# A two-layer hybrid encoder on Trainium2: the 64 rotary dimensions of a head side by side, one product for them in a score

## The chip, the core and the metric

The kernel runs on one core of one Trainium2 chip. The metric is the device time of one execution in microseconds (us). Engines: PE multiplies matrices (PEld is its weight load), DVE and ACT work on vectors, POOL and SP here only start transfers. Each engine works through its own queue in order and waits on semaphores.

## The reference, cut to what matters

Two layers of an encoder for 256 tokens of 2048 channels. Each layer has three branches (a state-space scan with a gated linear unit, a long convolution, and attention with latent queries and keys) that are gated, lifted, merged and normalised. The change touches only the attention:

```python
def apply_rope(x, pos):
    half = x.shape[-1] // 2                      # 32 of 64
    inv = ROPE_BASE ** (-jnp.arange(half, dtype=jnp.float32) / half)
    ang = pos.astype(jnp.float32)[:, :, None, None] * inv
    cos, sin = jnp.cos(ang), jnp.sin(ang)
    x1, x2 = xf[..., :half], xf[..., half:]
    return jnp.concatenate([x1 * cos - x2 * sin, x1 * sin + x2 * cos], axis=-1)

def mla_mixer(c_q, c_kv, k_r, pos, q_norm_g, w_uq, kv_norm_g, w_ukv):   # 8 heads
    q = (rms_norm(c_q, q_norm_g) @ w_uq).reshape(bsz, L, MLA_HEADS, 128 + 64)
    q = jnp.concatenate([q[..., :128], apply_rope(q[..., 128:], pos)], axis=-1)
    kv = (rms_norm(c_kv, kv_norm_g) @ w_ukv).reshape(bsz, L, MLA_HEADS, 128 + 128)
    k = jnp.concatenate([kv[..., :128], one apply_rope(k_r) for all heads], axis=-1)
    s = jnp.einsum('bqhd,bkhd->bhqk', q, k) * scale
    return jnp.einsum('bhqk,bkhd->bqhd', jax.nn.softmax(s, axis=-1), v)
```

## The kernel before

**Weights.** All large weights pass through SBUF in blocks of 1 MB: SP loads half blocks into a ring of four slots, ACT rounds a quarter of a block to WH, DVE subtracts to get the rest, WL, and PE multiplies with both. WH and WL hold one block: each quarter can be remade only when PE has used it (`parts_used`), and PE waits for the count that DVE adds for a finished WL quarter (`w_used`). ACT's splits are L398 and L404, DVE's are L417 (one quarter) and L426 (a whole block).

**The attention stage of a layer**, in PE's order: sums of squares for the two norms (L1912); the product of the gated linear unit (L1924); twelve query tiles, then eight key tiles (`three`, L1940), one quarter of a weight block for each, 12 products of 256 columns, evicted by ACT (L1463, L1469); the first product of the convolution's filter network (L1959); two blocks of V (L1969, 24 products of 512 columns each); the second product of the filter network (L1982); then eight heads. In a head PE makes two scores, one for each half of the queries (L1995 to L1997), one gated block of the next stage (`attention`, L1723), the transposes of the probabilities (L2005), a second gated block, the product with V (L2019), and a third gated block. The softmax runs meanwhile: DVE takes the maximum (L985), ACT the exponential (L1488), DVE the division (L993).

**The rotation.** Channels lie in rows (partitions), tokens in columns. The first 32 rotary dimensions of four heads fill one tile of 128 rows, the second 32 of the same heads another: `QR` has four tiles (two halves of eight heads), `PROJ` tiles 32 and 33 hold the key's two halves, each repeated four times. `rotate` (L919) makes the two rotated halves with six DVE instructions, four products, a difference and a sum, with `cosr` and `sinr` from `ROPE`. It is called once for the key, one tile wide, after the gating of the scan's output (L915), and once for the queries, two tiles wide, between the WL quarters of the second key block and those of the first V block. A score then adds three products: 128 rows without rotation, and 32 rows for each half:

```python
r = slice(32 * (h % 4), 32 * (h % 4) + 32)
release(mm(s, qn[:, h, tok], kn[:, h, :], start=True, stop=False))               # L1995
release(mm(s, qt[r, h // 4, tok], kt[r, 0, :], start=False, stop=False))         # L1996
done(mm(s, qt[r, 2 + h // 4, tok], kt[r, 1, :], start=False, stop=True), 4 + i)  # L1997
```

PE waits for both rotations (`qk_ready`) ahead of the first head.

**DVE's order there:** the gating (L909, L915), the key's rotation, eight WL quarters (the last four of Q, the first four of K), the low part of the scan's output (`YAL`, L940), four WL quarters, the queries' rotation, four WL quarters, a wait for `qk_ready`, then for each half of V a whole block of WL (L426) and the argument of a sine of the filter network (L958 and L543 to L548), then the heads.

**POOL** starts the transfers of the scan, and in this stage three small loads (W1, W2, the features; L510 to L512) once `YAL` is made, then the filter's biases and decays.

Of the kernel before, what the change touches and what calls it, by code (L numbers as in the profile page):

```python
# [34 lines left out]
P = 128  # L35
# [79 lines left out]
LAGS = 2 * STEP - 1  # L115
DVE_STEPS, DVE_S5_STEPS = 431, 21
SETUP_STEPS = 31
# [61 lines left out]
def trunk(nc, x, blocks, lp, ln, bc, w1, w2, b3, decay, feats, pT, pos, angles, consts, out):  # L179
    with ExitStack() as ctx:  # L180
        def sb(name, cols, parts=P, dt=F32):
            return ctx.enter_context(nc.sbuf_tensor(name, [parts, cols], dt))

        def sem(name):
            return ctx.enter_context(nc.semaphore(name))
# [8 lines left out]
        LNP = sb("LNP", 2 * DT)  # L194
        ANG = sb("ANG", 2)
        ROPE = sb("ROPE", 2 * T)
# [9 lines left out]
        def area(at, n):  # L206
            return ARENA[:, at * T:(at + n) * T]
# [58 lines left out]
        PR = area(71, 2)  # L266
        ROT = area(65, 4)
        ROOTS = [area(117 + i, 1) for i in range(4)]
        PT = area(89, 4)
        KT, VV = area(93, 4), area(97, 8)  # L270
# [33 lines left out]
        def tiles(buf, at, n, w=T):  # L304
            return buf[:, at:at + n * w].rearrange("p (n w) -> p n w", w=w)
# [31 lines left out]
        sq_ready, latent_ready, qk_ready = sem("sq_ready"), sem("latent_ready"), sem("qk_ready")  # L337
        max_ready, prob_ready = sem("max_ready"), sem("prob_ready")
        arg_ready, hid_ready = sem("arg_ready"), sem("hid_ready")
        taps_ready, abs_ready, ed_ready = sem("taps_ready"), sem("abs_ready"), sem("ed_ready")  # L340
# [112 lines left out]
        def _(pool):  # L453
# [6 lines left out]
            pool.sem_inc(y4_free, 1)  # L460
            with pool.Fori(0, DEPTH) as layer:
                pool.wait_ge(xh_ready, layer * GROUPS + GROUPS)
# [44 lines left out]


                pool.wait_ge(yl_ready, layer * 4 + 1)
                pool.dma_start(W1[0:33, :], w1[layer]).then_inc(late_loaded, 16)  # L510
# [45 lines left out]
        def _(dve):  # L556
# [61 lines left out]
            for layer in range(DEPTH):  # L618
# [299 lines left out]

                def rotate(x1, x2, n, o1, o2, t1, t2):  # L919
                    cb, sb_ = (c.unsqueeze(1).to_broadcast([P, n, T]) for c in (cosr, sinr))  # L920
                    st.did(v.tensor_tensor(t1, x1, cb, ALU.mult))
                    st.did(v.tensor_tensor(t2, x2, sb_, ALU.mult)); st.wait()
                    st.did(v.tensor_tensor(o1, t1, t2, ALU.subtract)); st.wait()
                    st.did(v.tensor_tensor(t1, x1, sb_, ALU.mult))
                    st.did(v.tensor_tensor(t2, x2, cb, ALU.mult)); st.wait()
                    v.tensor_tensor(o2, t1, t2, ALU.add).then_inc(qk_ready, 1)

                kt = tiles(KT, 0, 4)
                dve.wait_ge(rope_ready, 1)

                dve.wait_ge(glu_done, layer * 8 + 8)
                rotate(PROJt[:, 32:33, :], PROJt[:, 33:34, :], 1, kt[:, 0:1, :], kt[:, 1:2, :], kt[:, 2:3, :], kt[:, 3:4, :])
                qr, qt = tiles(QR, 0, 4), tiles(QT, 0, 4)

# [7 lines left out]
                dve.wait_ge(yl_ready, layer * 4 + 1)  # L942
                tq = tiles(ROT, 0, 4)
                for q in range(4):
                    make_wl_quarter(q, layer, after_k(q))
                rotate(qr[:, 0:2, :], qr[:, 2:4, :], 2, qt[:, 0:2, :], qt[:, 2:4, :], tq[:, 0:2, :], tq[:, 2:4, :])
                for q in range(4):
                    make_wl_quarter(q, layer, after_k(4 + q))


# [371 lines left out]
        def _(act):  # L1322
# [5 lines left out]
            act.wait_ge(pos_loaded, 32)  # L1328
            a.activation(ROPE[:, T:2 * T], U[:, 4 * T:5 * T], ACT.Sin)
            a.activation(ROPE[:, 0:T], U[:, 5 * T:6 * T], ACT.Sin, bias=half_pi, scale=-1.0).then_inc(rope_ready, 1)  # L1330
# [308 lines left out]
        def _(pe):  # L1639
# [5 lines left out]
            for layer in range(DEPTH):  # L1645
# [343 lines left out]
                for h in range(HEADS):  # L1989
                    r = slice(32 * (h % 4), 32 * (h % 4) + 32)  # L1990
                    for i in range(2):
                        s = bank[4 + i][:, 0:T]
                        tok = slice(i * P, (i + 1) * P)
                        take_bank(4 + i, "mla", 1 + h)
                        release(mm(s, qn[:, h, tok], kn[:, h, :], start=True, stop=False))  # L1995
                        release(mm(s, qt[r, h // 4, tok], kt[r, 0, :], start=False, stop=False))  # L1996
                        done(mm(s, qt[r, 2 + h // 4, tok], kt[r, 1, :], start=False, stop=True), 4 + i)  # L1997

                    attention = lambda k: gated_block("lifta", k // 6, k % 6, (xh, xl), (split(YAH, WT), split(YAL, WT)), lift_a(k))
                    attention(3 * h)  # L2000
                    take_bank(6, "mla", 1 + h)
                    for i in range(2):
                        pe.wait_ge(prob_ready, layer * 16 + (h * 2 + i + 1))
                        for kt_ in range(2):
                            ins = nc.tensor.transpose(bank[6][:, kt_ * T + i * P:kt_ * T + (i + 1) * P],  # L2005
                                                      PR[:, i * T + kt_ * P:i * T + (kt_ + 1) * P], ident)
                    done(ins, 6)
                    if h == 1:

                        pe.wait_ge(yl_ready, layer * 4 + 1)  # L2010
                    attention(3 * h + 1)

                    if h == 0:
                        for b in (2, 3, 7):
                            out_of(b, "mla", 0)
                    out_of(6, "mla", 1 + h)
                    take_bank(7, "mla", 1 + h)
                    for k in range(2):
                        ins = mm(bank[7][:, 0:T], VV[:, k * W + h * P:k * W + (h + 1) * P],  # L2019
                                 PT[:, (h % 2) * 2 * T + k * T:(h % 2) * 2 * T + (k + 1) * T], start=(k == 0), stop=(k == 1))  # L2020
                    done(ins, 7)
                    attention(3 * h + 2)
# [197 lines left out]
def weight_blocks(w_in, w_glu, w_uq, w_ukv, w3, w_lift, w_ple, w_out):  # L2220
# [8 lines left out]
    out += [block_of(column_tiles(w_in, seg(c_kv, m))) for m in range(4)]  # L2229
    out += [block_of(column_tiles(w_in, np.tile(np.arange(32), 4) + c_kr + 32 * i)) for i in range(2)]  # L2230
    out += [block_of(column_tiles(w_in, seg(z, m))) for z in (a_z, b_z, c_z) for m in range(WT)]
# [3 lines left out]
    q_cols = [192 * h + np.arange(P) for h in range(HEADS)]  # L2235
    for half in range(2):
        for g in range(2):
            q_cols.append((192 * heads[4 * g:4 * g + 4] + 128 + 32 * half + np.arange(32)).reshape(-1))
    out += [block_of(sum((column_tiles(w_uq, q_cols[m + i]) for i in range(4)), [])) for m in range(0, 12, 4)]
# [28 lines left out]
def shape_constants():  # L2268
# [19 lines left out]
    inv = np.float32(10000.0) ** (-np.arange(half, dtype=np.float32) / np.float32(half))  # L2288
    angles = np.stack([np.tile(inv, 4), np.full(P, HALF_PI, np.float32)], axis=1).astype(np.float32)

# [68 lines left out]
```

## Time and profile before

| | |
|---|---|
| runs | 2487.06 us, median of 3 (2485.95 to 2489.69) |
| the profiled execution | 2488.99 us, its span 2487.4 us |
| PE | busy 2423.8 us (97%), 15208 matrix instructions |
| DVE | busy 1832.8 us (74%) |
| ACT | busy 1227.9 us (49%) |
| POOL | busy 248.8 us (10%) |
| bytes moved | 413.73 MB, 166 GB/s over the span |
| PE's mean granted clock | 0.993 of full |

The span runs from the first to the last instruction of the profiled execution; a busy share is an average over stages that differ. One fp32 product appears as two matrix instructions. Times of instructions below are counted from the span's start; the first layer's attention stage lies at about 475 to 724 us, the second's at about 1708 to 1957 us.

### The profile page before, as it was taken

To read this page: it belongs to the slowest core of one execution; us is meant where nothing else is said; L and a number is where in the kernel's file an instruction comes from. 1 tells how busy PE (TensorE), PEld (TensorE's weight loads), DVE (VectorE), ACT (ScalarE), POOL (GpSimd) and SP (SyncE) were. 2 spreads that over 40 slices of the span, in tenths; PEclk is the share of its full clock that TensorE was granted. 3 is DMA by queue.
4 is the path that set the end of the run, shared out by engine and by line. 5 is a ranking of instruction groups with operands and counts; after the bars stand their busy time and mean duration, and the time that the engine had idled before them with its cause. 6 is when DMAs were issued, how large, how long until landed. Compare 5 with 4: busy or idle time off the path is not lost.

```text
span 2487.4 us, 43446 instructions
## 1 busy us (share of the span) xinstructions
PE 2423.8 (97%) x15208; PEld 2006.4 (81%) x15208; DVE 1832.8 (74%) x3207; ACT 1227.9 (49%) x2206; POOL 248.8 (10%) x478
## 2 busy tenths in 40 slices
PE   7999999999999999999999999999999999999998
PEld 6888888887776777898778888888877777778987
DVE  7888888677787876566678888886777777755665
ACT  5455555564443434453455555555644444344534
POOL 3421212100000000000043121111000000000000
PEclk9999999999999999999999999999999999999999
DMA  7555555444453435555565555554444534355553
GB/s 257 182 179 168 177 171 178 152 162 153 148 173 119 144 111 190 188 172 175 169 209 173 174 174 173 178 178 138 164 150 150 179 110 153 114 193 190 170 178 136
DMA packets 124317, 413.73 MB, mean 166 GB/s; under 512 B 19780, under 2 KB 25978, under 8 KB 123952
## 3 DMA queue, kind: packets, MB, share of 16 engines
q1 hardware_dynamic: 107136, 390.12, 47.5%
q0 software_dynamic: 17072, 22.18, 3.1%
q8 instruction: 66, 1.08, 0.2%
q14 instruction: 43, 0.35, 0.0%
HBM read 405.01 MB, written 7.21 MB: 166 GB/s over the span
## 4 chain that ended last, share of the span: by engine, by line
PE 94%; DVE 4%; issue 1%; ACT 1%; PEldq 0%; DMA 0%; PEld 0%; DVEq 0%; POOL 0%; ACTq 0%; POOLq 0%
PE bank L1723 31%; PE bank L1765 21%; PE bank L1767 10%; PE bank L2157 7%; PE bank L1698 5%; PE bank L2077 2%; PE bank L1924 2%; PE bank L1940 2%; PE bank L2091 1%; PE bank L2057 1%; PE bank L1680 1%; PE bank L1969 1%; PE bank L1996 1%; PE bank L1827 1%; PE bank L1995 1%
## 5 line engine op out<-in xcount | busy, mean ns | idle before, releaser
L398 ACT ACTIVATE WH<-ring 128x512 fp32r<-128x512 f32 x1376 | 862.4, 632 | 1118.7 <-PE bank L1723 472.1
L426 DVE TENSOR_TENSOR WL<-ring,WH 128x512 fp32r<-128x512 f32 x860 | 579.4, 689 | 419.3 <-ACT WH L398 416.5
L1765 PE MATMUL bank<-XX,WH 128*128 128x512 f32 x2304 | 833.8, 405 | 31.2 <-DVE XX L611 15.0
L1767 PE MATMUL bank<-XX,WL 128*128 128x256 f32 x2304 | 650.5, 282 | 0.0
L1765 PEld LDWEIGHTS bank<-XX,WH 128*128 128x128 f32 x2304 | 437.0, 190 | 143.9 <-issue 33.5
L1723 PE MATMUL bank<-WH,XX 128*128 128x512 f32 x1536 | 485.2, 397 | 4.4 <-issue 2.9
L417 DVE TENSOR_TENSOR WL<-ring,WH 128x512 fp32r<-128x512 f32 x556 | 379.1, 687 | 145.4 <-ACT WH L398 130.0
L1767 PEld LDWEIGHTS bank<-XX,WL 128*128 128x128 f32 x2304 | 439.5, 191 | 0.0
L1723 PEld LDWEIGHTS bank<-WH,XX 128*128 128x128 f32 x1536 | 285.0, 188 | 80.5 <-issue 21.6
L1723 PE MATMUL bank<-WL,XX 128*128 128x512 f32 x768 | 299.7, 390 | 0.0
L1723 PEld LDWEIGHTS bank<-WL,XX 128*128 128x128 f32 x768 | 144.1, 188 | 31.2
L1698 PE MATMUL bank<-XX,WH 128*128 128x256 f32 x640 | 115.9, 284 | 1.0 <-issue 1.0
L1698 PEld LDWEIGHTS bank<-XX,WH 128*128 128x128 f32 x640 | 99.7, 192 | 1.8 <-issue 1.8
L2157 PE MATMUL bank<-WH,MIXH 128*128 128x512 f32 x256 | 100.4, 392 | 0.0
L2157 PE MATMUL bank<-WL,MIXH 128*128 128x512 f32 x256 | 99.7, 389 | 0.0
L2157 PE MATMUL bank<-WH,MIXL 128*128 128x512 f32 x256 | 99.6, 389 | 0.0
L1698 PE MATMUL bank<-XX,WL 128*128 128x256 f32 x320 | 90.5, 283 | 0.0
L506 POOL DMA_DIRECT2D ARENA<-y_scratch x128 | 66.3, 518 | 82.1 <-DMA y_scratch<-ARENA 63.7
L494 POOL DMA_DIRECT2D ARENA<-lag_scratch x128 | 65.7, 513 | 76.8 <-DMA lag_scratch<-ARENA 55.9
L476 POOL DMA_DIRECT2D ARENA<-u_scratch x128 | 67.5, 528 | 15.1 <-issue 3.3
L1698 PEld LDWEIGHTS bank<-XX,WL 128*128 128x128 f32 x320 | 61.4, 192 | 0.0
L2077 PE MATMUL bank<-ARENA,CON 128*128 128x512 f32 x128 | 57.5, 597 | 0.7 <-issue 0.6
(333 smaller groups left out, 3270.9 us busy)
## 6 DMA issues: line engine op xcount, KB each, us to landing
ring<-in_blocks SPq DMA_DIRECT2D x736, 512.0 KB, 3.3
ARENA<-in_bc POOLq DMA_DIRECT2D x2, 2048.0 KB, 9.5
ARENA<-in_decay POOLq DMA_DIRECT2D x8, 512.0 KB, 4.1
ARENA<-in_x SPq DMA_DIRECT2D x4, 512.0 KB, 8.2
u_scratch<-ARENA POOLq DMA_DIRECT2D x16, 128.0 KB, 3.2
ARENA<-u_scratch POOLq DMA_DIRECT2D x128, 16.0 KB, 2.9
ARENA<-lag_scratch POOLq DMA_DIRECT2D x128, 16.0 KB, 2.6
y_scratch<-ARENA POOLq DMA_DIRECT2D x16, 128.0 KB, 3.4
```

The lines of the kernel that those rows point to most:

```text
L398: nc.scalar.activation(wh[q], raw(which[0], q), ACT.Copy).then_inc(wh_ready[q], 1)
L417: nc.vector.tensor_tensor(wl[q], raw(which[0], q), wh[q].bitcast(F32), ALU.subtract).then_inc(w_used[slot(which[0], q // 2)], 1)
L426: vec.tensor_tensor(wl[q], raw(which[0], q), wh[q].bitcast(F32), ALU.subtract).then_inc(w_used[slot(which[0], half)], 1)
L476: pool.dma_start(split(U4[rows, m * T:(m + 1) * T], 4), by_step[s_, t]).then_inc(u4_loaded, 16)
L494: pool.dma_start(split(M[rows, :], 4), by_half[s_][:, :, (STEP - 1 - t) * 16:(2 * STEP - 1 - t) * 16]).then_inc(m_ready, 16)
L506: pool.dma_start(split(U4[rows, bass.ds(ct * T, T)], STEP), by_group[q // 2, q % 2, g_]).then_inc(y_loaded, 16)
L1698: ins = mm(o, w_, x_, start=start and i == 0 and n == 0, stop=stop and i == 7 and n == 2)
L1723: ins = mm(bank[b][:, :], x_, w_[q], start=first and n == 0, stop=last and n == 2)
L1765: ins = mm(bank[b][:, :], h, xx[:, :, k, :], start=(k == 0), stop=(k == DT - 1), skip_group_check=True)
L1767: ins = mm(bank[b][:, 0:T], l, xh[:, k, :], start=False, stop=(k == DT - 1), skip_group_check=True)
L2077: ins = mm(bank[b][:, :], tab[:, t, m * P:(m + 1) * P], ZT[:, t * W + half * CW:t * W + (half + 1) * CW], start=(t == 0), stop=(t == 1))
L2157: ins = mm(bank[b][:, :], x_[:, k, token[t]], w_[q], start=False, stop=(k == 15 and n == 2), skip_group_check=True)
```

## The change

The 64 rotary dimensions of a head now lie in 64 neighbouring rows: a query tile holds two heads, and the key's tile holds the 64 dimensions twice. A second tile holds the same with the two halves of 32 swapped. Then the rotation is x * cos + swapped * (sin with a sign by row): three DVE instructions. For the key the swapped tile comes from the projection, with its weight columns in another order. For the queries POOL copies the four blocks of 32 rows of `QR` crosswise to `QS` by four transfers from SBUF to SBUF, 128 KB each, when all query tiles are out of PSUM and the memory of `QS` is free; DVE waits for them (`qs_loaded`) ahead of the queries' rotation, which now stands behind all eight WL quarters. A score has one product of 64 rows in place of two of 32. POOL's loop over the layers is written out.

```diff
-        ANG = sb("ANG", 2)
+        ANG = sb("ANG", 3)
...
-        ROT = area(65, 4)
...
-        PT = area(89, 4)
+        PT, QS = area(89, 4), area(89, 4)
...
-            with pool.Fori(0, DEPTH) as layer:
+            for layer in range(DEPTH):
...
+                for b in (0, 1):
+                    pool.wait_ge(psum_free[b], read_out(layer, "mla", b, 5))
+                pool.wait_ge(glu_done, layer * 8 + 8)
+                for r in range(4):
+                    into, of = 32 * r, 32 * (r ^ 1)
+                    pool.dma_start(QS[into:into + 32, :], QR[of:of + 32, :]).then_inc(qs_loaded, 16)
                 pool.wait_ge(yl_ready, layer * 4 + 1)
                 pool.dma_start(W1[0:33, :], w1[layer]).then_inc(late_loaded, 16)
...
-                def rotate(x1, x2, n, o1, o2, t1, t2):
+                def rotate(x, swapped, n, o):
                     cb, sb_ = (c.unsqueeze(1).to_broadcast([P, n, T]) for c in (cosr, sinr))
-                    st.did(v.tensor_tensor(t1, x1, cb, ALU.mult))
-                    st.did(v.tensor_tensor(t2, x2, sb_, ALU.mult)); st.wait()
-                    st.did(v.tensor_tensor(o1, t1, t2, ALU.subtract)); st.wait()
-                    st.did(v.tensor_tensor(t1, x1, sb_, ALU.mult))
-                    st.did(v.tensor_tensor(t2, x2, cb, ALU.mult)); st.wait()
-                    v.tensor_tensor(o2, t1, t2, ALU.add).then_inc(qk_ready, 1)
+                    st.did(v.tensor_tensor(o, x, cb, ALU.mult))
+                    st.did(v.tensor_tensor(swapped, swapped, sb_, ALU.mult)); st.wait()
+                    v.tensor_tensor(o, o, swapped, ALU.add).then_inc(qk_ready, 1)
...
-                rotate(PROJt[:, 32:33, :], PROJt[:, 33:34, :], 1, kt[:, 0:1, :], kt[:, 1:2, :], kt[:, 2:3, :], kt[:, 3:4, :])
+                rotate(PROJt[:, 32:33, :], PROJt[:, 33:34, :], 1, kt[:, 0:1, :])
...
                 for q in range(4):
                     make_wl_quarter(q, layer, after_k(q))
-                rotate(qr[:, 0:2, :], qr[:, 2:4, :], 2, qt[:, 0:2, :], qt[:, 2:4, :], tq[:, 0:2, :], tq[:, 2:4, :])
                 for q in range(4):
                     make_wl_quarter(q, layer, after_k(4 + q))
+                dve.wait_ge(qs_loaded, layer * 64 + 64)
+                rotate(qr, qs, 4, qt)
...
-            a.activation(ROPE[:, T:2 * T], U[:, 4 * T:5 * T], ACT.Sin)
+            a.activation(ROPE[:, T:2 * T], U[:, 4 * T:5 * T], ACT.Sin, scale=ANG[:, 2:3])
...
-                    r = slice(32 * (h % 4), 32 * (h % 4) + 32)
+                    r = slice(64 * (h % 2), 64 * (h % 2) + 64)
...
-                        release(mm(s, qt[r, h // 4, tok], kt[r, 0, :], start=False, stop=False))
-                        done(mm(s, qt[r, 2 + h // 4, tok], kt[r, 1, :], start=False, stop=True), 4 + i)
+                        done(mm(s, qt[r, h // 2, tok], kt[r, 0, :], start=False, stop=True), 4 + i)
...
-    out += [block_of(column_tiles(w_in, np.tile(np.arange(32), 4) + c_kr + 32 * i)) for i in range(2)]
+    out += [block_of(column_tiles(w_in, np.tile(np.roll(np.arange(64), 32 * i), 2) + c_kr)) for i in range(2)]
...
-    for half in range(2):
-        for g in range(2):
-            q_cols.append((192 * heads[4 * g:4 * g + 4] + 128 + 32 * half + np.arange(32)).reshape(-1))
+    for h in range(0, HEADS, 2):
+        q_cols.append((192 * heads[h:h + 2] + 128 + np.arange(64)).reshape(-1))
...
+    sign = np.tile(np.repeat([-1.0, 1.0], half), 2)
```

## Rows read from the trace of the kernel before

**Rows 1.** The page's part 1: PE's busy us, share of the span, instructions.

```profile
PE 2423.8 (97%) x15208; PEld 2006.4 (81%) x15208; DVE 1832.8 (74%) x3207; ACT 1227.9 (49%) x2206; POOL 248.8 (10%) x478
```

**Rows 2.** Windows, V, then heads, first layer: us; busy by engine; clock; DMA share.

```profile
544.00:556.00 12.00, 12.00 (x52) 9.47 (x52) 7.95 (x16) 7.00 (x12) 0.00 (x0) 1.00 0.54 176
...
562.00:724.00 162.00, 162.00 (x710) 127.69 (x709) 120.77 (x253) 79.71 (x142) 1.58 (x3) 1.00 0.46 153
```

**Rows 3.** Timeline of PE, fourth head, first layer: start, us, line, operands, count.

```profile
620.36 0.69 PE L1996 MATMUL bank<-ARENA 32*128 32x256 f32 x2
620.90 0.59 PE L1997 MATMUL bank<-ARENA 32*128 32x256 f32 x2
621.42 0.70 PE L1995 MATMUL bank<-ARENA 128*128 128x256 f32 x2
622.05 0.69 PE L1996 MATMUL bank<-ARENA 32*128 32x256 f32 x2
```

**Rows 4.** Timeline of PE, both layers, gated unit to first head; [idle before].

```profile
504.70 6.42 PE L1924 MATMUL bank<-ARENA,ring 128*128 128x256 f32 x29
...
524.54 0.35 PE L1940 MATMUL bank<-CH,WH 128*128 128x256 f32 x1 [1.91 <-DVE WL L417]
...
1783.24 0.39 PE L1969 MATMUL bank<-WH,CH 128*128 128x512 f32 x1
...
1788.77 0.70 PE L1982 MATMUL bank<-ARENA 64*128 64x256 f32 x2
1789.40 0.70 PE L1995 MATMUL bank<-ARENA 128*128 128x256 f32 x2
...
1798.35 0.60 PE L2005 MATMUL bank<-CON,ARENA 128*128 128x128 f32 x4
1798.71 0.71 PE L1723 MATMUL bank<-WH,XX 128*128 128x512 f32 x2
```

**Rows 5.** Timelines of DVE and PE, seventh head, first layer: probabilities done, transposes.

```profile
690.38 0.36 DVE L993 TENSOR_SCALAR ARENA<-ARENA,SM 128x256 f32<-128x256 f32 x1
...
692.10 0.60 PE L2005 MATMUL bank<-CON,ARENA 128*128 128x128 f32 x4
```

**Rows 6.** Timeline of DVE, both layers: rotations, splits, first head's softmax.

```profile
505.19 1.23 DVE L903 TENSOR_TENSOR CL<-ARENA,CH 128x1024 fp32r<-128x1024 f32 x1
...
522.57 0.42 DVE L924 TENSOR_TENSOR ARENA<-ARENA,ROPE 128x256 f32<-128x256 f32 x1
...
523.71 2.64 DVE L417 TENSOR_TENSOR WL<-ring,WH 128x512 fp32r<-128x512 f32 x4
...
1772.89 0.69 DVE L921 TENSOR_TENSOR ARENA<-ARENA,ROPE 128x512 f32<-128x512 f32 x1
...
1778.95 0.69 DVE L417 TENSOR_TENSOR WL<-ring,WH 128x512 fp32r<-128x512 f32 x1 [0.18 <-ACT WH L404]
...
1797.32 0.35 DVE L993 TENSOR_SCALAR ARENA<-ARENA,SM 128x256 f32<-128x256 f32 x1
1797.64 2.50 DVE L426 TENSOR_TENSOR WL<-ring,WH 128x512 fp32r<-128x512 f32 x4
```

**Rows 7.** Windows behind PE's stall in either layer; columns as in rows 2.

```profile
525.90:529.30 3.40, 3.40 (x19) 3.40 (x18) 1.14 (x2) 1.35 (x4) 0.00 (x0) 0.52 0.83 265
...
1757.00:1762.00 5.00, 3.09 (x26) 2.91 (x26) 4.04 (x9) 1.92 (x4) 0.00 (x0) 1.00 0.25 85
```

**Rows 8.** Timelines of ACT and POOL, second layer: last query eviction, next load.

```profile
1765.15 0.38 ACT L1463 ACTIVATE ARENA<-bank 128x256 f32<-128x256 f32 x1 [0.54 <-PE bank L1940]
...
1770.98 0.54 POOL L510 DMA_DIRECT2D ARENA<-in_w  x1 [49.62 <-DVE YAL L940]
```

**Rows 9.** DMA view: issues, KB each, median us from issue to landing.

```profile
u_scratch<-ARENA POOLq DMA_DIRECT2D x16, 128.0 KB, 3.2
...
ARENA<-in_pos POOLq DMA_DIRECT2D x1, 128.0 KB, 4.8
```

More of the change, by code:

```diff
@@ L115 @@
 LAGS = 2 * STEP - 1
-DVE_STEPS, DVE_S5_STEPS = 431, 21
+DVE_STEPS, DVE_S5_STEPS = 425, 21
 SETUP_STEPS = 31
@@ L338, in trunk @@
         max_ready, prob_ready = sem("max_ready"), sem("prob_ready")
+        qs_loaded = sem("qs_loaded")
         arg_ready, hid_ready = sem("arg_ready"), sem("hid_ready")
@@ L931, in _ @@
                 dve.wait_ge(glu_done, layer * 8 + 8)
-                rotate(PROJt[:, 32:33, :], PROJt[:, 33:34, :], 1, kt[:, 0:1, :], kt[:, 1:2, :], kt[:, 2:3, :], kt[:, 3:4, :])
-                qr, qt = tiles(QR, 0, 4), tiles(QT, 0, 4)
+                rotate(PROJt[:, 32:33, :], PROJt[:, 33:34, :], 1, kt[:, 0:1, :])
+                qr, qt, qs = tiles(QR, 0, 4), tiles(QT, 0, 4), tiles(QS, 0, 4)
                 for m in range(4, 12):
@@ L942, in _ @@
                 dve.wait_ge(yl_ready, layer * 4 + 1)
-                tq = tiles(ROT, 0, 4)
                 for q in range(4):
                     make_wl_quarter(q, layer, after_k(q))
-                rotate(qr[:, 0:2, :], qr[:, 2:4, :], 2, qt[:, 0:2, :], qt[:, 2:4, :], tq[:, 0:2, :], tq[:, 2:4, :])
                 for q in range(4):
                     make_wl_quarter(q, layer, after_k(4 + q))
+                dve.wait_ge(qs_loaded, layer * 64 + 64)
+                rotate(qr, qs, 4, qt)
                 dve.wait_ge(qk_ready, layer * 2 + 2)
@@ L2288, in shape_constants @@
     inv = np.float32(10000.0) ** (-np.arange(half, dtype=np.float32) / np.float32(half))
-    angles = np.stack([np.tile(inv, 4), np.full(P, HALF_PI, np.float32)], axis=1).astype(np.float32)
+    sign = np.tile(np.repeat([-1.0, 1.0], half), 2)
+    angles = np.stack([np.tile(inv, 4), np.full(P, HALF_PI, np.float32), sign], axis=1).astype(np.float32)
     n_ch = 2 * W
```

## The prediction, made before the change was run

> **What bounds the kernel now.** I read the page's busy times first: PE is busy for nearly the whole span [rows 1], so only work that leaves PE, or a stall of PE that goes, can shorten it. Then I split the span by stages with the view of windows: during the V products and during the eight attention heads PE is busy in every microsecond, with DVE at two thirds to three quarters [rows 2]. The timelines of PE and DVE around those stages then show what each edit meets, and the waits say what ends last there.
>
> **The scores.** A score is three fp32 products of 256 columns, each two instructions. A head holds two scores: the first rotary product starts 0.54 us before the second, the second 0.52 us before the next score's full-height product, and that one 0.63 us before the next rotary product [rows 3]. In a run of full-height fp32 products of that size, 29 instructions take 6.42 us, the last 0.38 of them its own length, so two cost 0.43 us [rows 4]. So what exceeds 0.43 us belongs to going from 128 rows to few rows and back: about 0.10 us at each change and 0.10 us more on the first product behind it. The change leaves one product of 64 rows between two of 128. The trace has such a one: L1982, 64 rows, stands alone among full products, and the next starts 1789.40 - 1788.77 = 0.63 us later [rows 4]. The pair of rotary products cost 0.54 + 0.52 = 1.06 us, the one will cost 0.63: 0.43 us less for a score, 0.86 us for a head.
>
> The Trainium skill (TensorEngine Tiling (Array Packing), Key Properties) says that changing the tiling mode, unlike changing the tile, drains the engine. By that rule the product that goes takes no drain with it, and the saving is its bare time in a run of its own kind, and the trace agrees with 0.43 us; without the rule one would credit its whole distance, and the sum would be that of rival E below.
>
> The bounds of this term: at 0.53 a score, 1.06 a head; at nothing, if 64 rows cost what two times 32 rows did. L1982's row is nearest, so I take 0.86.
>
> Does PE get to use it? In heads 1 to 7 the nearest thing is the softmax, which must be done when the transposes start. The tightest head that I found is the seventh of the first layer: the last normalised probabilities are there at 690.38 + 0.36 = 690.74, the transposes start at 692.10 [rows 5]; 0.86 earlier is 691.24, still 0.50 behind. So 7 x 0.86 = 6.0 us a layer. In head 0 it is tighter. There DVE still does the sines of the filter network, a chain that starts with PE's second half of V and not with the scores: only then can ACT split the last quarter of V's block, DVE subtract it and go on to the first sine. In the second layer its softmax ends at 1797.32 + 0.35 = 1797.67 [rows 6]; PE starts the transposes at 1798.35 and the next gated block at 1798.71 [rows 4]. That block needs the first WL quarter, which DVE begins at 1797.64 [rows 6] and ends 0.69 later; PE goes on 0.14 us after such an end, as it did at 524.54 after a quarter that began at 523.71 [rows 4, 6]. So the block can start at 1797.64 + 0.69 + 0.14 = 1798.47 at best: 0.24 of the 0.86 us is kept, and PE waits for the rest.
>
> **The key's rotation.** Three of six DVE instructions go. In the first layer L924 to L926 fill 522.57 to 523.71, 1.14 us [rows 6], and the short wait for L923 ahead of them goes as well. I take 1.2 us. This is on the path: PE sat idle 1.91 us until the WL quarter right behind this rotation [rows 4]. The idle shrinks to 0.7 us; what ends last there is the same quarter. Both layers have that order, so 1.2 us each.
>
> In the first layer the granted clock was 0.52 of full in 525.9 to 529.3, just behind that stall: 3.4 us at the lower level, 1.2 GHz, worth 1.6 us. In the second layer the same stall was followed by 1.00 [rows 7]. With a stall of a third of the length I count the 1.6 us as won, once; the bound is nothing.
>
> **The queries' rotation** becomes three DVE instructions of 1024 elements instead of six of 512, and moves behind four more WL quarters. A two-input instruction of that size took 1.23 us [rows 6]; three, the first overlapped by 0.08 us with its neighbour, the last awaited to its end since the wait on qk_ready is now right behind it, make 3.6 us. Before, the rotation began at 1772.89 [rows 6] while PE was still in the K products. Now it begins behind the quarter that starts at 1778.95, so at about 1778.95 + 0.61 = 1779.56, and ends at 1783.16. Queued behind it on DVE are the four WL quarters of the second V block; the first ends at 1783.85, and with 0.14 us PE sees it at 1783.99. PE wants it at 1783.24, where its second half of V starts, the 25th of 48 instructions [rows 4]. So PE stands 0.75 us here, a new stall in each layer. Bounds: by 2 x 0.69 for a thousand elements the rotation is 4.2 us and the stall 1.3; were two of the three to overlap more, 0.5. The next quarters take 0.69 us each, and PE needs (1788.77 - 1783.24) / 4 = 1.4 us for one, so nothing else is late. The quarters of the first V block, which stood behind the rotation, come sooner; PE did not wait for them. The scores wait for qk_ready only 6 us after this.
>
> **The four transfers.** POOL issues them when the last query tile is out of PSUM, in the second layer at 1765.15 + 0.38 = 1765.53. It has nothing else until the loads of W1, W2 and the features at 1770.98 [rows 8]; four issues like that one's 0.54 us, with gaps, end near 1768.0, so those three are not moved. On SP nothing is moved. What the trace lacks is a copy from SBUF to SBUF. The nearest rows move 128 KB as well: 3.2 us to landing from SBUF to DRAM, 4.8 us for the positions from DRAM [rows 9]. The last of the four, issued at 1767.4, lands at 1770.6 to 1772.2. DVE asks for it at 1779.56, behind YAL and all eight quarters of K and the first V block: 7 us of cover, made of those and of PE's K products. I cost them at nothing. If that cover were gone, each microsecond past 1779.56 would stop DVE, then WL of V, then PE, by that microsecond.
>
> Without cost, each for one reason: the layer loop of POOL written out (the queue still waits for the same producers), the sign in the sine's scale (one instruction at the start), the host's order of weights (same blocks), and 1 MB more traffic in 413 MB.
>
> **Sum.** A layer: 6.0 + 0.24 + 1.2 - 0.75 = 6.7 us; two layers 13.4; the clock 1.6; together 15.0. The profiled execution took 2488.99 us (span 2487.4 and 1.6 around it), so it would take 2474.0. The median of the runs is 1.93 lower, 2487.06, and so I forecast 2472.
>
> **Rivals.** A, the attention stage stops being PE's: DVE fills 120.77 of 162 us there [rows 2] and runs in order, so every head could end as head 0 does, with 0.24 us. For it speaks only head 0, against it the 1.36 us between softmax and transposes in the tightest later head. A layer then gives 8 x 0.24 + 1.2 - 0.75 = 2.4, in all 4.8 + 1.6 = 6.4 us: 2480.7.
>
> B, the transfers are late. If each took 4.8 us and they went one behind the other, the last would land at 1765.6 + 19.2 = 1784.8, 5.2 us past 1779.56: 10.4 us lost in two layers, 2482.5, within 0.2%. At 3.2 us each they would land at 1778.4, and nothing would be lost. The Trainium skill (DMA: Bandwidth & Descriptors, Rules for kernel authors) says that transfers to separate groups of partitions serialize, since all run on the same engines. No run so far shows that for these four; read strictly, it makes this rival the time to expect.
>
> C, the other side: the same transfers land so late that the change loses. It decides when half of the 15.0 us, 7.5, is lost in each layer: at a landing 21.5 us after the first issue. From 24 us after it the kernel is slower by over 5 us, near 2493. No row is near that: the longest landing in the rows is a fifth of it, and the DMA share is about half in these stages [rows 2].
>
> D, the one product of 64 rows costs as much as two of 32, so that the change does not do what it says: 2 x (1.2 - 0.75) + 1.6 = 2.5 us remain, 2484.6, within 0.2%. L1982's row speaks against it.
>
> E, a removed product saves its whole distance, 1.06 us a head: 2 x 7 x 0.20 = 2.8 us more, 2469.3.
>
> **How the numbers follow.** Forecast 0.62, E 0.16, A 0.08, B 0.05, D 0.04, C 0.05. Changes of 0.2% (5 us) are about what a measurement of this kernel can tell from no change. Faster by that: 0.62 + 0.16 + 0.08 = 0.86; same 0.05 + 0.04 = 0.09 (B, D); slower 0.05 (C). At the low end the range takes in E with the stall at its lower bound (2 x 0.25 us) and one more stretch of clock like that of 1.6 us: 2467. At the high end it takes in A: 2481. It leaves out B at its worst, D and C. The forecast's own range, with the clock not won and the stall at its upper bound, is 2470 to 2475.
>
> **What would show it.** Right: 64 fewer matrix instructions on PE; scores at 2.41 us from first start to next block instead of 3.26; a head period down by 0.86; a PE wait of 0.7 us instead of 1.9 for WL at the third query block; a new PE wait of about 0.75 us for WL at the second half of V; a PE wait of some 0.6 us in head 0; DVE never waiting for the transfers. Wrong: a DVE wait ended by a DMA before the rotation, PE waits for probabilities in later heads, or a 64-row product taking over 0.8 us.

## The result, and the profile after

The changed kernel takes 2472.02 us, the median of three runs (2471.87 to 2473.47), against 2487.06 before: a ratio of 0.9939 with an interval of [0.9926, 0.9953], 15.0 us faster. Its profiled execution took 2472.02 us with a span of 2470.4.

Part 1 of the page of the kernel after, which answers to [rows 1]:

```profile
PE 2407.2 (97%) x15144; PEld 1993.0 (81%) x15144; DVE 1829.0 (74%) x3195; ACT 1226.3 (50%) x2206; POOL 251.2 (10%) x486
```

PE has 64 instructions less (two layers, eight heads, two scores, one product of two instructions each) and 16.6 us less busy time, nearly all of the 17.0 us by which the span is shorter. It is the bound as before. The line numbers move a little: the score's products are L1998 and L1999, V's L1972, the three-product tiles' L1943, the gated block's L1726, the rotation L927 to L929, the transfers L514.

Windows of V and of the heads, first layer, columns as in [rows 2]:

```profile
541.00:553.00 12.00, 11.38 (x49) 8.89 (x49) 9.42 (x16) 6.22 (x11) 0.00 (x0) 1.00 0.51 169
560.00:717.00 157.00, 156.77 (x683) 122.82 (x681) 121.45 (x253) 79.10 (x143) 1.55 (x3) 1.00 0.50 161
```

In V PE is now idle for 0.62 of 12 us, where it was idle for nothing; in the heads for 0.23 us in all.

The timeline of PE in the fourth head of the first layer (start, length, line, operands, count; compare [rows 3]):

```profile
615.45 0.59 PE L1998 MATMUL bank<-ARENA 128*128 128x256 f32 x2
615.97 0.70 PE L1999 MATMUL bank<-ARENA 64*128 64x256 f32 x2
616.60 0.70 PE L1998 MATMUL bank<-ARENA 128*128 128x256 f32 x2
617.23 0.70 PE L1999 MATMUL bank<-ARENA 64*128 64x256 f32 x2
617.85 0.50 PE L1726 MATMUL bank<-WH,XX 128*128 128x512 f32 x1
```

Starts are 0.52, 0.63, 0.63 and 0.62 us apart: the two scores take 2.40 us, where the prediction has 2.41 for now and 3.26 for before.

The timeline of PE at the landmarks of the first layer, before and then after, in brackets the idle time before an instruction and what ended it:

```profile
510.77 0.47 PE L1940 MATMUL bank<-CH,WH 128*128 128x256 f32 x1
...
544.59 0.49 PE L1969 MATMUL bank<-WH,CH 128*128 128x512 f32 x1
...
555.70 0.70 PE L1982 MATMUL bank<-ARENA 64*128 64x256 f32 x2
...
577.57 0.59 PE L1995 MATMUL bank<-ARENA 128*128 128x256 f32 x2
...
598.69 0.59 PE L1995 MATMUL bank<-ARENA 128*128 128x256 f32 x2
...
726.04 1.14 PE L2039 MATMUL bank<-ARENA 64*128 64x512 f32 x4 [0.37 <-issue]
```

```profile
510.27 0.47 PE L1943 MATMUL bank<-CH,WH 128*128 128x256 f32 x1
...
522.80 0.36 PE L1943 MATMUL bank<-CH,WH 128*128 128x256 f32 x1 [0.66 <-DVE WL L417]
...
541.36 0.50 PE L1972 MATMUL bank<-WH,CH 128*128 128x512 f32 x1
...
547.71 0.47 PE L1972 MATMUL bank<-WH,CH 128*128 128x512 f32 x1 [0.61 <-DVE WL L426]
...
553.33 0.70 PE L1985 MATMUL bank<-ARENA 64*128 64x256 f32 x2
...
562.14 0.60 PE L2007 MATMUL bank<-CON,ARENA 128*128 128x128 f32 x4
562.95 0.73 PE L1726 MATMUL bank<-WH,XX 128*128 128x512 f32 x2 [0.21 <-DVE WL L426]
...
574.90 0.59 PE L1998 MATMUL bank<-ARENA 128*128 128x256 f32 x2
...
595.16 0.59 PE L1998 MATMUL bank<-ARENA 128*128 128x256 f32 x2
...
717.35 0.71 PE L2041 MATMUL bank<-ARENA 64*128 64x512 f32 x2 [0.37 <-issue]
```

These starts give the account, in us of the first layer; the last column has the same stretches of the second, read in the same way:

| stretch (starts of) | before | after | won | forecast | second layer, won |
|---|---|---|---|---|---|
| first query tile to first V product | 510.77 to 544.59 | 510.27 to 541.36 | 2.73 | 1.2 + 1.6 of clock | 1.28 |
| V, to the filter network's second product | to 555.70 | to 553.33 | -0.86 | -0.75 | -0.91 |
| head 0, to the scores of head 1 | to 577.57 | to 574.90 | 0.30 | 0.24 | 0.32 |
| heads 1 to 7, to the tap product L2041 | to 726.04 | to 717.35 | 6.02 | 6.0 | 5.99 |

A head's period is 595.16 - 574.90 = 20.26 us, as the next one to 615.45 is; before it was 598.69 - 577.57 = 21.12: 0.86 less. The first layer gives 8.2 us, the second 6.7 (its norm products start 10.3 us earlier than before, the end of its heads comes 16.9 earlier). The rest of the 16.97 us by which the two profiled executions differ lies where nothing was changed: 0.5 us ahead of 510 us, and 1.6 between the two attention stages, where before PE's clock was lower for longer. The 0.5 us hide a loss. From the norms' first product to the first query tile, the same 145 instructions, the windows are, before and then after:

```profile
479.80:510.80 31.00, 31.00 (x145) 27.31 (x145) 15.81 (x27) 18.14 (x23) 4.11 (x8) 1.00 0.34 118
```

```profile
477.60:510.30 32.70, 32.70 (x145) 28.57 (x145) 15.80 (x27) 18.11 (x23) 4.11 (x8) 0.95 0.31 112
```

After the change the lower clock stands here and costs 1.7 us; behind the stall it is gone. The medians differ by 15.04.

What ends PE's idle time, over the whole span (total, times, longest):

```profile
PE bank L1726 <- DVE WL L426: 1.9, 4, 0.8
PE bank L1943 <- DVE WL L417: 1.3, 2, 0.7
PE bank L1972 <- DVE WL L426: 1.2, 2, 0.6
```

The first was 1.6 in two times before; the two new ones are head 0's, 0.21 and 0.20 us. The second was 3.8, the 1.91 us of [rows 4] in each layer. The third is new.

The timeline of DVE around both rotations and of POOL at the transfers, first layer, and the transfers' group in the DMA view (KB each, median us to landing):

```profile
520.83 0.43 DVE L927 TENSOR_TENSOR ARENA<-ARENA,ROPE 128x256 f32<-128x256 f32 x1
...
521.97 2.64 DVE L417 TENSOR_TENSOR WL<-ring,WH 128x512 fp32r<-128x512 f32 x4
...
543.23 1.22 DVE L927 TENSOR_TENSOR ARENA<-ARENA,ROPE 128x1024 f32<-128x1024 f32 x1
...
546.88 1.29 DVE L426 TENSOR_TENSOR WL<-ring,WH 128x512 fp32r<-128x512 f32 x2
...
529.87 2.01 POOL L514 DMA_DIRECT2D ARENA<-ARENA  x4 [44.55 <-ACT ARENA L1466]
...
ARENA<-ARENA POOLq DMA_DIRECT2D x8, 128.0 KB, 4.1
```

From the first key instruction to the WL quarter behind the rotation are 1.14 us, and from the first query instruction to the quarter behind it 3.65. No idle time stands ahead of 543.23: DVE does not wait for the transfers. They are issued 0.5 us apart and landed 2.2, 3.3, 5.1 and 5.5 us after their issues, so the last by 529.87 + 1.5 + 5.5 = 536.9, 6.3 us before DVE asks.

### The profile page after: what moved, and what is told of

The parts are those of the page before. It is cut to its first block, busy times and chain, and to the rows that moved or that the text cites. A ratio compares the mean times of both kernels' runs of the same rounds, so it can differ in the third digit from the quotient of the medians.

```text
span 2470.4 us, 42952 instructions
## 1 busy us (share of the span) xinstructions
PE 2407.2 (97%) x15144; PEld 1993.0 (81%) x15144; DVE 1829.0 (74%) x3195; ACT 1226.3 (50%) x2206; POOL 251.2 (10%) x486
## 4 chain that ended last, share of the span: by engine, by line
PE 93%; DVE 4%; issue 1%; ACT 1%; PEldq 0%; DMA 0%; PEld 0%; DVEq 0%; POOL 0%; ACTq 0%; POOLq 0%
PE bank L1726 31%; PE bank L1768 21%; PE bank L1770 10%; PE bank L2159 7%; PE bank L1701 5%; PE bank L2079 2%; PE bank L1927 2%; PE bank L1943 2%; PE bank L2093 1%; PE bank L2059 1%; PE bank L1683 1%; PE bank L1999 1%; PE bank L1830 1%; PE bank L1998 1%; PE bank L2041 1%
## 5 line engine op out<-in xcount | busy, mean ns | idle before, releaser
L1726 PE MATMUL bank<-WH,XX 128*128 128x512 f32 x1536 | 485.8, 398 | 5.0 <-issue 3.0
L1726 PEld LDWEIGHTS bank<-WH,XX 128*128 128x128 f32 x1536 | 285.3, 188 | 81.5 <-issue 21.9
L1726 PE MATMUL bank<-WL,XX 128*128 128x512 f32 x768 | 300.1, 391 | 0.0
L1726 PEld LDWEIGHTS bank<-WL,XX 128*128 128x128 f32 x768 | 144.3, 188 | 30.8
```

The costliest lines, as they stand in the source:

```text
L1726: ins = mm(bank[b][:, :], x_, w_[q], start=first and n == 0, stop=last and n == 2)
```

## The experiments

All are edits of the changed kernel, or that kernel once more. Four were run beside a kernel before that took 2487.03 us, the other four beside one that took 2488.12.

**What does a product of 64 rows cost beside one of 32?** The 64-row product is made twice, so that a score has as many products as before:

```diff
                         release(mm(s, qn[:, h, tok], kn[:, h, :], start=True, stop=False))
+                        release(mm(s, qt[r, h // 2, tok], kt[r, 0, :], start=False, stop=False))
                         done(mm(s, qt[r, h // 2, tok], kt[r, 0, :], start=False, stop=True), 4 + i)
```

> The changed kernel with the 64-row product of every score issued twice (the rotary part is counted twice, so the output is another). Theory: a further product of the same height costs its bare 0.43 us, since the price of going from 128 rows to 64 and back is paid once however many products stand between. A head grows by 0.86 us in heads 1 to 7; in head 0 PE already stands about 0.5 us behind DVE, so only about 0.3 shows there. 2 x (7 x 0.86 + 0.3) = 12.6 us more than the changed kernel: about 2484.6 us. Rival, a product costs its whole distance of 0.53 us: 2 x (7 x 1.06 + 0.5) = 15.8, about 2488. Rival, the heads are bound by DVE: less than 5 us more.

It took 2485.94 us, ratio 0.9995 [0.9986, 1.0005], 1.3 us above the theory and 2 below the rival. The timeline of PE in its fourth head:

```profile
618.51 0.70 PE L1999 MATMUL bank<-ARENA 64*128 64x256 f32 x2
619.05 0.59 PE L2000 MATMUL bank<-ARENA 64*128 64x256 f32 x2
619.57 0.70 PE L1998 MATMUL bank<-ARENA 128*128 128x256 f32 x2
```

Behind each of the two 64-row products the distance, 0.54 and 0.52, is that behind the 32-row pair in [rows 3] to the hundredth. A product of 64 rows costs what one of 32 rows costs, and the gain of the scores is the number of products. Rival D is out. Two products of 32 rows in the new layout were not tried.

**What does the change of height cost?** The 64-row product is replaced by a second full-height one:

```diff
                         release(mm(s, qn[:, h, tok], kn[:, h, :], start=True, stop=False))
-                        done(mm(s, qt[r, h // 2, tok], kt[r, 0, :], start=False, stop=True), 4 + i)
+                        done(mm(s, qn[:, h, tok], kn[:, h, :], start=False, stop=True), 4 + i)
```

> The changed kernel with the 64-row product replaced by a second full-height product of the same columns (queries and keys without rotation twice; the rotary part is left out of the scores, so the output is another). Instructions on PE are as many as in the changed kernel. Theory: what a change of height costs goes: 0.2 us for each of two scores in a head and 0.2 for the way back, twice: a score is 0.43 + 0.43 us, a head 0.8 us shorter, 5.3 to 5.6 us a layer (the seventh head has only 0.5 us of slack to its softmax, and head 0 gains nothing): about 2461.2 us. Rival, there is no price on the change of height and a small product costs what a full one does: 2472.

It took 2462.89 us, ratio 0.9905 [0.9889, 0.9922]. The timeline of PE in its fourth head:

```profile
614.81 0.59 PE L1998 MATMUL bank<-ARENA 128*128 128x256 f32 x2
615.24 0.59 PE L1999 MATMUL bank<-ARENA 128*128 128x256 f32 x2
615.67 0.59 PE L1998 MATMUL bank<-ARENA 128*128 128x256 f32 x2
```

Now the distances are 0.43 us, and the head's period is 614.81 - 595.35 = 19.46 us, 0.80 less than after. A head after the change goes four times from one height to the other, so each such step costs 0.20 us. That is the split which the prediction read from [rows 3] and [rows 4]: 0.43 us for a product, the rest for the changes of height. It is also why the change saves 0.43 and not 0.53 us a score: it leaves as many changes of height as there were. Rival E is out. The rule of the Trainium skill that the prediction weighed (TensorEngine Tiling (Array Packing), Key Properties) agrees; it gives no figure, and the trace has 0.20 us. Of 14 x 0.80 = 11.2 us in heads 1 to 7 of both layers, 10.0 arrived in the profiled execution and 9.1 by the medians. What the trace lacks is the seventh head's, which gains only 0.1 us in either layer, where the expectation allowed it 0.5. The timelines of DVE and of PE there, first layer:

```profile
680.63 2.50 DVE L426 TENSOR_TENSOR WL<-ring,WH 128x512 fp32r<-128x512 f32 x4
```

```profile
680.35 0.81 PE L2007 MATMUL bank<-CON,ARENA 128*128 128x128 f32 x4
681.38 0.74 PE L1726 MATMUL bank<-WH,XX 128*128 128x512 f32 x2 [0.22 <-DVE WL L426]
```

The block behind the transposes starts 1.03 us after them in place of 0.36, at the end of the WL quarter that DVE makes behind the softmax. One head in seven has become DVE's.

**What does a late transfer cost?** The four transfers move behind the loads of W1, W2 and the features and behind the last key tile:

```diff
+                pool.wait_ge(yl_ready, layer * 4 + 1)
+                pool.dma_start(W1[0:33, :], w1[layer]).then_inc(late_loaded, 16)
...
                 for b in (0, 1):
-                    pool.wait_ge(psum_free[b], read_out(layer, "mla", b, 5))
+                    pool.wait_ge(psum_free[b], read_out(layer, "mla", b, 9))
...
-                pool.wait_ge(yl_ready, layer * 4 + 1)
-                pool.dma_start(W1[0:33, :], w1[layer]).then_inc(late_loaded, 16)
...
```

> The changed kernel with the four transfers issued later: behind the loads of W1, W2 and the features, and only when all key tiles are out of PSUM (at about 541.2 in the first layer). Theory: the cover of about 7 us is then used up. The last transfer is issued near 542.9 and lands 4.1 us later, near 547, 3.8 us after DVE asks for it at 543.2. DVE then WL of the second V block then PE are late by that: PE's wait at the second half of V grows from 0.6 to about 4.4 us, 2 x 3.8 = 7.6 us in all: about 2479.6 us, and up to 3 us more if the granted clock falls behind the longer stall. Rival, the landing of the transfers is not what DVE waits for, or PE has other slack there: 2472, no DVE wait ended by a DMA.

It took 2485.28 us, ratio 0.9996 [0.9986, 1.0006]: 13.3 us more than the change, above the expected 7.6 and the 3 that were allowed for the clock. The timelines of DVE and then of PE in the first layer:

```profile
548.80 1.22 DVE L927 TENSOR_TENSOR ARENA<-ARENA,ROPE 128x1024 f32<-128x1024 f32 x1 [3.75 <-DMA ARENA<-ARENA]
```

```profile
553.30 0.76 PE L1972 MATMUL bank<-WH,CH 128*128 128x512 f32 x1 [4.45 <-DVE WL L426]
...
558.12 0.63 PE L1972 MATMUL bank<-WL,CH 128*128 128x512 f32 x1
558.55 0.54 PE L1972 MATMUL bank<-WH,CH 128*128 128x512 f32 x1
...
561.56 0.70 PE L1985 MATMUL bank<-ARENA 64*128 64x256 f32 x2
```

DVE waits 3.75 us for a DMA, and PE's wait grows from 0.61 to 4.45 us: 3.84, so lateness is passed on one for one, as the prediction has it. What it lacked comes behind. The second half of V lasts 561.56 - 553.30 = 8.26 us, after the change 553.33 - 547.71 = 5.62. In the windows of this kernel the granted clock is 0.58 in 1780 to 1785 us, around the end of the second layer's wait, and in the first layer:

```profile
555.00:560.00 5.00, 5.00 (x15) 3.90 (x15) 3.79 (x10) 3.44 (x6) 0.00 (x0) 0.61 0.63 202
```

Products that start 0.23 us apart at 2.4 GHz start 0.43 apart at 1.2 GHz until 558.55: 2.64 us more. With 3.84 that is 6.5 us. In the second layer PE's wait is 4.18 us and the half lasts 8.03, together 6.0 more; so 12.5 in all, against 13.3 measured. So rivals B and C have the right mechanism with too low a price, and C would have decided sooner than they say: at this lateness of 3.75 us the whole gain is almost gone.

**Can the rotations leave the path?** The key's rotation moves behind the fourth of the eight WL quarters which follow it, the queries' behind the first quarter of V's first block:

```diff
-                dve.wait_ge(glu_done, layer * 8 + 8)
-                rotate(PROJt[:, 32:33, :], PROJt[:, 33:34, :], 1, kt[:, 0:1, :])
...
                 for m in range(4, 12):
                     make_wl_quarter(m % 4, layer, after_q(m))
+                    if m == 7:
+                        dve.wait_ge(glu_done, layer * 8 + 8)
+                        rotate(PROJt[:, 32:33, :], PROJt[:, 33:34, :], 1, kt[:, 0:1, :])
...
                 for q in range(4):
                     make_wl_quarter(q, layer, after_k(4 + q))
-                dve.wait_ge(qs_loaded, layer * 64 + 64)
-                rotate(qr, qs, 4, qt)
+                    if q == 0:
+                        dve.wait_ge(qs_loaded, layer * 64 + 64)
+                        rotate(qr, qs, 4, qt)
```

> The changed kernel with both rotations moved on DVE: the key's behind the first four WL quarters after the gating instead of ahead of them, the queries' behind the first WL quarter of the first V block instead of behind its last. Theory: both stand on PE's path only by their place. PE's waits of 0.66 us at the third query block and of 0.61 us at the second half of V go, with about 0.15 us each around them: 2 x 1.4 = 2.8 us less, about 2469.2 us; the two waits in the first head stay. Rival, the waits move: DVE is late with the first key block's or the second V block's later quarters and PE stands there instead, 2472.

It took 2469.14 us, ratio 0.9929 [0.9913, 0.9946]. In its view of waits no tile of the three-product helper and no V product waits for WL any more, so 2.5 us of PE's idle time are gone, and the transfers, asked for some 7 us sooner, are still in time. The timeline of DVE:

```profile
536.28 1.22 DVE L927 TENSOR_TENSOR ARENA<-ARENA,ROPE 128x1024 f32<-128x1024 f32 x1
```

The changed kernel and this one were then run again beside each other:

> The changed kernel itself once more, as the base that the next three are compared with on one chip: about 2472 us, between 2470 and 2474 by the scatter of its three runs, PE's waits at the third query block, at the second half of V and in head 0 as before.

> The kernel with both rotations moved into gaps of DVE, once more beside the changed kernel. Theory: 2 x 1.4 = 2.8 us below the changed kernel on the same chip. Rival: below by less than 1 us, the difference of the first run being one of granted clock.

They took 2471.95 us (ratio 0.9937 [0.9924, 0.9951]) and 2470.97 us (0.993 [0.9916, 0.9943]): 1.0 us apart, where 2.8 was expected. The waits are gone in this trace too. The starts of the first query tile, the first V product and the filter network's second product in its first layer:

```profile
511.93 0.47 PE L1945 MATMUL bank<-CH,WH 128*128 128x256 f32 x1
...
542.13 0.50 PE L1974 MATMUL bank<-WH,CH 128*128 128x512 f32 x1
...
553.24 0.70 PE L1987 MATMUL bank<-ARENA 64*128 64x256 f32 x2
```

These two stretches take 30.20 and 11.11 us, to 0.02 us the same in the other layer and in the first trace of this edit; in both traces of the changed kernel they take 31.08 and 11.97. So 1.74 us a layer are won where the edit was made, 3.5 in all. The time as a whole doesn't show them: the spans of the edit's two profiled executions, 2463.8 and 2469.4 us, differ by more, all of it where nothing was edited, and their mean clocks are 0.996 and 0.994. In the second, the windows of 15 us from 1245, 1290 and 1695 us are at 0.89 and that from 30 us at 0.92, where the changed kernel's trace beside it has 1.00; only that from 480 us is the other way round, 1.00 against 0.89. A window at 0.89 costs 0.11 x 15 = 1.65 us.

**Can head 0 be freed?** On top of the last edit, the second sine's argument (six DVE instructions), the clearing of B3 and ACT's sine move behind the first convolution step of head 0:

```diff
-                    round_phase(dve, st, *ARG, arg_ready)
-                dve.wait_ge(arg_ready, layer * 2 + 2)
-                v.memset(B3, 0.0).then_inc(b3_cleared, 1)
+                    if i == 0:
+                        round_phase(dve, st, *ARG, arg_ready)
...
                     short_conv(3 * h)
+                    if h == 0:
+                        round_phase(dve, st, *ARG, arg_ready)
+                        dve.wait_ge(arg_ready, layer * 2 + 2)
+                        v.memset(B3, 0.0).then_inc(b3_cleared, 1)
```

> The kernel with both rotations moved into gaps, and the second sine of the filter network (six DVE instructions, a memset and ACT's sine) moved from ahead of head 0's softmax to behind its first convolution tile. Theory: in head 0 PE waits because DVE works off that sine's argument before it comes to the maximum, so PE's two waits there, 0.54 us together, go and nothing takes their place, since DVE has 4 us to spare in a head: 2 x 0.54 = 1.1 us below the kernel with the rotations in gaps, about 3.9 below the changed one. Rival: the work moved makes DVE late for the second or third gated block of head 0 or for head 1's softmax, and PE waits there instead: no difference to the kernel with the rotations in gaps.

It took 2471.14 us (0.9934 [0.992, 0.9948]), no gain: the expectation's rival came true. Of the waits of its PE:

```profile
PE bank L2030 <- DVE ARENA L1006: 1.1, 2, 0.5
```

Head 0's two waits for WL are gone (the gated block's are 1.6 us in two times again, as before the change), but the product with V (L2030) now waits 0.5 us in each layer for the probabilities' copy (L1006), which stands on DVE behind the moved work. The wait changed its place, and head 0 grew by 0.3 us in each layer.

**Is the low clock behind the key's rotation tied to its length?** Three idle DVE instructions stand ahead of the key's rotation, as many as the change removed:

```diff
                 dve.wait_ge(glu_done, layer * 8 + 8)
+                cb, sb_ = (c.unsqueeze(1).to_broadcast([P, 1, T]) for c in (cosr, sinr))
+                st.did(v.tensor_tensor(kt[:, 1:2, :], PROJt[:, 32:33, :], sb_, ALU.mult))
+                st.did(v.tensor_tensor(kt[:, 2:3, :], PROJt[:, 33:34, :], cb, ALU.mult)); st.wait()
+                st.did(v.tensor_tensor(kt[:, 3:4, :], kt[:, 1:2, :], kt[:, 2:3, :], ALU.add)); st.wait()
                 rotate(PROJt[:, 32:33, :], PROJt[:, 33:34, :], 1, kt[:, 0:1, :])
```

> The changed kernel with three more DVE instructions of 256 elements ahead of the key's rotation, so that it is as long as before the change (six); their result is not used. Theory: PE's wait at the third query block goes back from 0.66 to about 1.9 us in both layers, 2 x 1.2 = 2.4 us more than the changed kernel, and the granted clock may fall behind that stall as it did in one layer of two before: 0 to 3.2 us more on top. Rival: this rotation is not on PE's path, no difference.

It took 2476.69 us, ratio 0.9954 [0.9939, 0.9969]. One row of its waits and its window behind the stall of the first layer:

```profile
PE bank L1947 <- DVE WL L417: 3.8, 2, 1.9
```

```profile
525.00:540.00 15.00, 12.89 (x105) 12.50 (x105) 10.56 (x16) 9.45 (x19) 3.30 (x7) 1.00 0.63 176
```

The wait is that of before to the tenth, so the three instructions are what it was made of. But the clock stays at 1.00 behind it, in the second layer too. Beside the changed kernel of the same call the time is 4.7 us longer, and its fastest run (2475.40 us) is slower than that kernel's slowest (2473.64); the waits account for 2.5. The spans of the two profiled executions differ by 5.5 us. Of these, 2.5 lie between the first query tile and the first V product, 1.26 and 1.27 in the two layers, and 2.9 between the norms' first product and the first query tile, ahead of the three instructions. There the window of the first layer is:

```profile
479.60:513.50 33.90, 33.90 (x145) 29.38 (x145) 15.80 (x27) 18.06 (x23) 4.10 (x8) 0.91 0.31 107
```

The changed kernel's trace of the same call has 32.7 us there, and in the second layer 31.0 where this one has 32.7. So behind the longer stall nothing was lost to the clock, in either layer; the excess lies in front of it, in the same stretch that differs between before and after.

## Why the prediction was right, point by point

**The scores** were right in place and size: 0.86 us a head, 6.02 of 6.0 us in heads 1 to 7. The first two experiments show why: a product costs the same with 64 rows as with 32, and the changes of height, which stay, cost 0.20 us each. The prediction's check on whether PE could use it held too: in the seventh head the last probabilities are ready at 683.77 and the transposes start at 684.27, 0.50 us behind, as forecast. But this was not the nearest wait. As in head 0, the block behind the transposes needs the WL quarter that DVE makes behind the softmax:

```profile
683.74 2.50 DVE L426 TENSOR_TENSOR WL<-ring,WH 128x512 fp32r<-128x512 f32 x4
```

```profile
684.63 0.71 PE L1726 MATMUL bank<-WH,XX 128*128 128x512 f32 x2
```

The quarter ends at 683.74 + 0.69 = 684.43, and where PE waits for such a quarter it goes on 0.06 us later (680.63 + 0.69 = 681.32 to 681.38 in the kernel of full height), so the slack was 684.63 - 684.43 - 0.06 = 0.14 us and not 0.50. The prediction asked this of head 0 alone; that 0.86 us still fitted into the seventh head was luck, and the kernel of full height shows it used up. So heads 1 to 7 stayed PE's, and rival A is out, in the seventh head by little.

**Head 0** kept 0.30 us where 0.24 was forecast, for the reason given: the gated block starts 0.81 us after the transposes instead of 0.36 [rows 4], waiting for the WL quarter behind the softmax. PE went on about 0.06 us after the quarter and not 0.14 as the prediction took it.

**The key's rotation** took 1.25 us off the stall (1.91 to 0.66), forecast 1.2 and 0.7, and putting three instructions back restored 1.9.

**The queries' rotation** made the one new stall, 0.61 us in each layer; the V stage as a whole lost 0.86 in the first, the term was 0.75. Its three instructions took 3.65 us on DVE, forecast 3.6. This term could have been avoided by place, not by length: behind another WL quarter it costs no wait.

**The transfers** were hidden. The last landed at most 7.0 us after the first issue, with 6.3 us of cover left (forecast 7). The Trainium skill's rule that transfers to separate groups of partitions serialize (DMA: Bandwidth & Descriptors, Rules for kernel authors) agrees with the landings as far as they go: issued 0.5 us apart, the four were there at 532.1, 533.7, 536.0 and 536.9, one behind the other. Whether each waited for the one before or they shared the engines, landings alone don't tell. What is refuted is the price that rival B put on it, 4.8 us each. That lateness would be passed on one for one, the late transfers show; that it brings some 2.5 us of low clock with it, the prediction didn't see, and so its rivals B and C were priced too low.

**The clock's 1.6 us** is the weak term. In the stretch behind the stall it came true: that is at 1.00 after the change. But the lower clock now stood ahead of the query tiles, in the second of the two windows above, and cost 1.7 us there; from the norms' first product to the first V product the first layer won 1.05 us. And with the old stall put back the clock stayed at 1.00 behind it in both layers; of four stalls of 1.9 us, two before and two there, one was followed by a low clock. So the term is not shown to be something that the change removes; it belongs to what differs between executions. The steps that are the change's own give 2.73 - 1.5 of clock - 0.86 + 0.30 + 6.02 = 6.7 us in the first layer and 6.7 in the second, 13.4 as forecast. In the second layer no clock is in the account. That the medians differ by 15.04 and not 13.4 is left to the clock, and only argued; 13.4 would lie within the interval of the measured ratio as well. In the later comparison nine runs of the kernel before have a mean granted clock of 0.9929 and five of the changed kernel 0.9946; 0.0017 of 2470 us is 4.2 us, an estimate of the most that this difference is worth, so there is room for the 1.6. That the forecast met the median to the tenth is luck: without its clock term it would have been 2473.7.

**The best version** that was run has the rotations in the gaps: 2469.14 and 2470.97 us, below both kernels by the medians, and as a whole time clearly so only below the one before; stretch by stretch it is 3.5 us below the changed one.

## What to carry to other kernels

Price a removed matrix product by its distance in a run of its own kind, and the changes of height beside it on their own: they stay as long as one short product stands between full ones. Where an instruction of an engine in order grows, look first for the place in its queue with slack: moved by a few instructions, the same work costs nothing. When one head of several is checked for slack, check every wait in it, the weights' as well as the data's. A stall of several microseconds on PE is to be priced with the lower clock that can follow it, and a clock term read from one execution isn't to be credited to a change; where the clock scatters by more than the gain, compare the edited stretches, start to start.

## What the runs showed of the hardware

An fp32 product of 256 columns costs 0.43 us at full height, and at 32 or 64 rows 0.43 us as well with 0.20 us for each change between few rows and 128. With stalls of 4.45 and 4.18 us the granted clock fell to the lower level both times, by the end of the stall; behind stalls of 1.9 us once in four; behind those of 0.6 to 0.7 us not once in the traces here. The stall of 2.9 us ahead of the norms' products is the same in all ten traces, in both layers: behind it the stretch to the first query tile took 31.0 us ten times, 32.7 nine times and 33.9 once. Four copies of 128 KB from SBUF to SBUF, issued within 2.0 us, landed in 2.2 to 5.5 us (median 4.1), and in 2.7 us (median) where they were issued later. Between executions of one kernel the low-clock stretches change their place; the two profiled executions of the rotations in the gaps differ by 5.6 us in this way.
